# Sums of squares on VectorE, moved transposes, gates and loads, and unread matmuls in two seams of a two-block transformer kernel

## What is computed

```
# block 1
u = rmsnorm(x); p_fox, p_rwkv = u @ w_in
mix = [forgetting_attention(p_fox), rwkv7_time_mix(p_rwkv)] @ w_out
h = x + rmsnorm(mix);  z = rmsnorm(h)
h = h + rmsnorm((silu(z @ w_gate) * (z @ w_up)) @ w_down)
# block 2
h2 = rmsnorm(h); hq, hf, hi, hg, rq, rk, rv, rg, gate_a, gate_b = h2 @ w_in_2
o_hg  = head_rms(hgrn2(hq, hf, hi, lower_bounds)) * w * silu(hg)      # 8 heads of 128
o_ret = head_rms(retention(rotary(rq), rotary(rk), rv)) * silu(rg)    # 4 heads, values of 512
merged = sigmoid(gate_a) * (o_hg @ w_a) + sigmoid(gate_b) * (o_ret @ w_b)
x = h + merged @ w_out_2
x = x + peer_ffn(rmsnorm(x))       # 16384 experts, 8 x 16 chosen per token
return rmsnorm(x)
```

## Time and profile before

| what | us |
|---|---|
| runs | 3435.29, 3425.33, 3425.12 |
| median | 3425.33 |
| the profiled execution, its own time | 3432.69 |
| its span in the trace | 3430.9 |
| PE busy | 3323.2 (97%) |
| DVE busy | 1903.7 (55%) |
| ACT busy | 1251.6 (36%) |
| DMA | 408 MB, mean 119 GB/s |

### The profile page before, as it was taken

How to read it: one execution, slowest core, us unless ns; L and a number is a source line. 1 busy time by engine, 2 the same in 40 slices (tenths; PEclk the granted TensorE clock), 3 DMA queues, 4 the chain that set the end, 5 groups by cost and what they waited for, 6 DMA issues and landing times.

```text
span 3430.9 us, 50060 instructions
## 1 busy us (share of the span) xinstructions
PE 3323.2 (97%) x18511; PEld 2707.1 (79%) x18511; DVE 1903.7 (55%) x3709; ACT 1251.6 (36%) x1622; POOL 131.7 (4%) x54
## 2 busy tenths in 40 slices
PE   8999999999799999989999999999999999999998
PEld 6676877878577788878878888888887788888886
DVE  4466446442565533342344999988884444444443
ACT  3333233322455333342333333444553333333332
POOL 0000000000000000000000445000000000000000
PEclk9999999999899999999999999999999999999999
DMA  3110013323222222213332444555556655555542
GB/s 135 58 44 2 4 49 98 98 92 98 74 67 73 80 74 73 73 62 98 94 100 80 146 144 141 158 179 183 184 183 220 209 192 194 196 196 193 192 146 80
DMA packets 146028, 408.31 MB, mean 119 GB/s; under 512 B 11224, under 2 KB 43992, under 8 KB 143584
## 3 DMA queue, kind: packets, MB, share of 16 engines
q1 hardware_dynamic: 73520, 265.85, 25.5%
q10 hardware_dynamic: 72368, 140.68, 11.3%
HBM read 337.28 MB, written 69.21 MB: 118 GB/s over the span
## 4 chain that ended last, share of the span: by engine, by line
PE 85%; DVE 11%; ACT 2%; issue 1%; ACTq 1%; DMA 1%; DVEq 0%; SPq 0%
PE bank L333 24%; PE bank L335 23%; PE bank L334 23%; PE bank L929 2%; PE bank L429 2%; PE bank L927 2%; PE bank L362 1%; PE bank L863 1%; ACT arena L970 1%; DVE arena L1961 1%; DVE arena L1924 1%; DVE arena L1925 1%; DVE arena L1927 1%; DVE arena L1959 1%; DVE arena L1926 1%
## 5 line engine op out<-in xcount | busy, mean ns | idle before, releaser
L333 PE MATMUL bank<-xs,ring_hi 128*128 128x512 f32 x2488 | 998.1, 401 | 38.3 <-DVE xs L1454 11.8
L335 PE MATMUL bank<-xs,ring_lo 128*128 128x512 f32 x2488 | 974.3, 392 | 0.0
L334 PE MATMUL bank<-xs,ring_hi 128*128 128x512 f32 x2488 | 973.7, 391 | 0.0
L970 ACT ACTIVATE ring_hi<-ring 128x1024 fp32r<-128x1024 f32 x503 | 531.6, 1059 | 660.8 <-DMA ring<-weights 427.0
L970 ACT ACTIVATE arena<-bank 128x512 f32<-128x512 f32 (+4 forms) x584 | 392.0, 705 | 1013.5 <-PE bank L335 727.4
L1488 DVE TENSOR_TENSOR ring_lo<-ring,ring_hi 128x1024 fp32r<-128x1024 f32 x246 | 299.9, 1224 | 566.0 <-ACT ring_hi L970 564.9
L333 PEld LDWEIGHTS bank<-xs,ring_hi 128*128 128x128 f32 x2488 | 470.4, 189 | 149.8 <-issue 27.0
L335 PEld LDWEIGHTS bank<-xs,ring_lo 128*128 128x128 f32 x2488 | 469.8, 189 | 101.6
L334 PEld LDWEIGHTS bank<-xs,ring_hi 128*128 128x128 f32 x2488 | 471.0, 189 | 99.9 <-issue 5.5
L1974 DVE TENSOR_TENSOR ring_lo<-ring,ring_hi 128x1024 fp32r<-128x1024 f32 x206 | 252.3, 1225 | 385.7 <-ACT ring_hi L970 385.7
L333 PE MATMUL bank<-gw,ring_hi 128*128 128x512 f32 x1024 | 398.5, 389 | 0.7 <-ACT arena L970 0.7
(11 more groups left out here) (279 smaller groups left out, 3391.2 us busy)
## 6 DMA issues: line engine op xcount, KB each, us to landing
ring<-weights SPq DMA_DIRECT2D x503, 512.0 KB, 3.6
hidden<-arena ACTq DMA_DIRECT2D x128, 256.0 KB, 4.1
gates<-arena ACTq DMA_DIRECT2D x16, 2048.0 KB, 6.7
arena<-hidden ACTq DMA_DIRECT2D x16, 2048.0 KB, 10.4
arena<-gates ACTq DMA_DIRECT2D x16, 2048.0 KB, 17.2
xres<-x_t ACTq DMA_DIRECT2D x4, 512.0 KB, 6.8
out_t<-arena SPq DMA_DIRECT2D x4, 512.0 KB, 3.0
arena<-ret_decay ACTq DMA_DIRECT2D x1, 1024.0 KB, 5.6
```

The lines of the kernel that those rows point to most:

```text
L333: pe.matmul(out_, wh, x[0], start=start, stop=False, skip_group_check=True)
L334: pe.matmul(out_, wh, x[1], start=False, stop=False, skip_group_check=True)
L335: return pe.matmul(out_, wl, x[0], start=False, stop=stop, skip_group_check=True)
L970: return act.activation(out_, in_, f, **kw)
```

## The change

1. *Sums of squares on DVE.* For norms 0, 1, 3 and 5 (`ACC`) DVE adds the squares (`add_square`) in a third buffer and PE does a single sum (`added_sum`). The same in retention: squares go to `SQ` and, in turn, two buffers at `SQ2`; DVE adds them between its splits of blocks 11 to 13, and one sum stands behind product 11. The values use banks 7 and 5 in turn, values 0 and 1 stand together before product 9, values 2 and 3 before products 10 and 11.
2. *Start.* Products 0 and 1 come before the sum of norm 0; the splits of blocks 2 and 3 stand ahead of the reciprocal.
3. *Fox loop.* The transposes of `TA` and `TB` for pairs 0 to 2 move from the late chain into units 19, 20, 23, 24, 27, 28, with ACT's copies one unit later. Ten tiles stay late; counters that named 36 now name 30.
4. *Seams.* `seam_clock` puts 12 unread matmuls behind the sum of norm 1 and 16 behind that of norm 4.
5. *Lower bounds.* Their softmax stands at the start of the down stage instead of behind it, on DVE and ACT.
6. *Merge.* The sigmoids of the first two gates and the splits of blocks 3 and 4 stand at copies 9 and 14 of the 24.
7. *Loads.* The four transfers stand before blocks 4, 5, 7 and 9 of the rest of U; that loop is unrolled.

The diff, without the renumbered counters:

```diff
+        ACC = {0: 62, 1: 73, 3: 20, 5: 20}
...
+            def seam_clock(n, b, count):
+
+                r = n % RING
+                for _ in range(count):
+                    pe.matmul(bank[b][:, :], ring_hi[:, r, 0:P], ring_hi[:, r, 0:T], start=True, stop=True, skip_group_check=True)
...
+            def added_sum(i):
+
+                pe.wait_ge(sq_used, (KD - 1) * (i + 1))
+                pe.matmul(bank[SUMS[i]][:, :], cc("ones"), tile(ACC[i]), start=True, stop=True,
+                          skip_group_check=True).then_inc(sum_ready, 1)
...
             for n in range(N_FOX):
                 product(n, [(n, KD)], XS, chunk_wait=xs_chunks(0) if n == 0 else None)
-                if n == 0:
+                if n == 1:
                     pe.wait_ge(in_cst, 16)
-                    norm_sums(0, KD)
+                    added_sum(0)
...
+                if u in (19, 20, 23, 24, 27, 28):
+                    i, g0 = (u - 19) % 4, (u - 19) // 4
+                    pe.wait_ge(rw_dve, 2 * g0 + 2)
+                    if 2 * g0 + i:
+                        pe.wait_ge(tok_out, 2 * g0 + i)
+                    for g in range(TT):
+                        tr = pe.transpose(bank[1][:, g * P:(g + 1) * P], tile((TA, TB)[i] + g0)[:, g * P:(g + 1) * P], cc("ident"))
+                    tr.then_inc(tok_ready, 1)
                 if u in (17, 21, 25, 29):
                     pe.wait_ge(rw_dve, 2 * m + 1)
+                    if m:
+                        pe.wait_ge(tok_out, 2 * m)
                     pe.matmul(bank[1][:, :], cc("bones"), tile(RKR), start=True, stop=True).then_inc(rw_pe, 1)
...
-            for i, (src, _) in enumerate(((TA, MA), (TB, MB), (TK, MK), (RV, MV))):
-                for m in range(NPAIR):
-                    j = 4 * i + m
+            pe.wait_ge(tok_out, 2 * (NPAIR - 1))
+            late = [(TA, 3), (TB, 3)] + [(TK, m) for m in range(NPAIR)] + [(RV, m) for m in range(NPAIR)]
+            for j, (src, m) in enumerate(late):
                     if j >= 2:
...
-                for k in {4: (0, 1), 5: (2, 3), 7: (4, 5, 6, 7)}.get(b, ()):
-                    norm_sum(1, k)
+            added_sum(1)
+            ready(B_FFN)
+            seam_clock(B_FFN, 5, 12)
...
-                if k:
-                    norm_sum(3, k - 1)
-            norm_sum(3, KD - 1)
+            added_sum(3)
             norm_sums(4, KD)
+            ready(B_HG)
+            seam_clock(B_HG, 5, 16)
...
+                def values(j):
+
                     if j == 0:
                         pe.wait_ge(rt_dve, h * 12 + 1 + 8)
                         pe.wait_ge(rt_act, h * 9 + 4)
...
+                    if j >= 2:
+                        pe.wait_ge(rt_act, h * 9 + 4 + j - 1)
+                    b = bank[(7, 5)[j % 2]]
...
+
+                product(q + 8, [(B_RET + 8, KD)], XS, h, 12, 12)
+                values(0)
+                for j in range(1, 4):
+                    values(j)
+                    product(q + 8 + j, [(B_RET + 8 + j, KD)], XS, h, 12, 12)
+                pe.wait_ge(rt_sum, h * 4 + 4)
+                pe.matmul(bank[4][:, :], cc("ones"), tile(R_["SQ"]), start=True, stop=True).then_inc(rt_pe, 1)
...
-                if k:
-                    norm_sum(5, k - 1)
...
                 if k == 0:
-                    norm_sum(5, KD - 1)
+                    added_sum(5)
...
+                added = i in ACC
+                if k >= 2 + added:
+                    act.wait_ge(sq_used, (KD - 1) * i + k - 1 - added)
+                elif i and k < 2:
                     act.wait_ge(root_used, i)
-                A(tile(NORM[i][0] + k % 2), src(k), ACT.Square).then_inc(sq_ready, 1)
+                A(tile(ACC[i] if added and k == 0 else NORM[i][0] + k % 2), src(k), ACT.Square).then_inc(sq_ready, 1)
...
+            dense(3)
             norm_root(0)
-            for n in range(3, N_FOX):
+            for n in range(4, N_FOX):
...
+                if u in (20, 21, 24, 25, 28, 29):
+                    i, g0 = (u - 20) % 4, (u - 20) // 4
+                    act.wait_ge(tok_ready, 2 * g0 + i + 1)
+                    A(tile((MA, MB)[i] + g0), bank[1][:, :], ACT.Copy).then_inc(tok_out, 1)
...
             act.wait_ge(ffn_pair, KF + 2)
+            act.wait_ge(lb_ready, 1)
+            A(lbt[:, 1:3, :], lbt[:, 1:3, :], ACT.Exp).then_inc(lb_ready, 1)
...
+                def gate(j):
+
                     act.wait_ge(block_used, h * 12 + B_RET + 8 + j + 1)
                     A(tile(R_["G"] + j), bank[(q + 8 + j) % NBANK][:, :], ACT.Silu).then_inc(evac, 1)
                     dense(B_RET + 8 + j + 3, h, 12)
-                    act.wait_ge(rt_pe, h * 16 + 8 + 2 * j + 1)
-                    st.go(A(arena[:, bass.ds(h * 4 + (ORET + j), 1), :].rearrange("p a t -> p (a t)"), bank[7][:, :], ACT.Copy))
-                    A(tile(R_["SQ"]), bank[7][:, :], ACT.Square).then_inc(rt_act, 1)
...
+                gate(0)
+                for j in range(4):
+                    b = bank[(7, 5)[j % 2]]
+                    act.wait_ge(rt_pe, h * 13 + 8 + j + 1)
+                    st.go(A(arena[:, bass.ds(h * 4 + (ORET + j), 1), :].rearrange("p a t -> p (a t)"), b[:, :], ACT.Copy))
+                    if j >= 2:
+                        act.wait_ge(rt_sum, h * 4 + j)
+                    A(tile(R_["SQ"] if j == 0 else SQ2 + j % 2), b[:, :], ACT.Square).then_inc(rt_act, 1)
+                    if j:
+                        gate(j)
...
+            def merge_gate(j):
+
+                act.wait_ge(block_used, B_MERGE + j + 1)
+                A(tile(MGT + j), bank[(q + j) % NBANK][:, :], ACT.Sigmoid).then_inc(evac, 1)
+                dense(B_MERGE + j + 3)
 
             for k in range(24):
                 if k == 9:
                     act.wait_ge(rt_dve, 12 * RET_H + 1)
+                    merge_gate(0)
+                if k == 14:
+                    merge_gate(1)
                 A(OHL[k][0], tile(OHG + k), ACT.Copy).then_inc(o_hi_ready, 1)
+            q += 2
...
-            def load(g, it=0):
+            def load_part(g, part, it=0):
 
...
-                if g > 1:
-                    act.wait_ge(ex_lo, it * 2 * JG + (g - 1) * JG)
...
+                if part == 0:
...
+            def load(g, it=0):
+
+                act.wait_ge(ex_lo, it * 2 * JG + (g - 1) * JG)
+                load_part(g, 0, it)
+                load_part(g, 1, it)
...
-            load(0)
-            load(1)
-            with act.Fori(1, NU_REST // 4 - 1) as i:
-                for b in range(4):
-                    expert_hi(n + b, i, 4)
-                    gelu(B_U + j0 + b, q + b, j0 + b, i, 4)
+            for b in range(4, NU_REST - 4):
+                if b in (4, 5):
+                    load_part(0, b - 4)
+                if b in (7, 9):
+                    load_part(1, (b - 7) // 2)
+                expert_hi(n + b)
+                gelu(B_U + j0 + b, q + b, j0 + b)
...
+            def add_square(i, k):
+
+                ve.wait_ge(sq_ready, KD * i + k + 1)
+                if k > 1:
+                    ve.wait_ge(sq_used, (KD - 1) * i + k - 1)
+                TTN(tile(ACC[i]), tile(ACC[i]), tile(NORM[i][0] + k % 2), ALU.add).then_inc(sq_used, 1)
...
             dense(1)
+            dense(2)
+            for k in range(1, KD):
+                add_square(0, k)
+            dense(3)
...
+            for n in range(B_WOUT + 4, B_FFN - 1):
                 dense(n)
-            for b in range(3):
-                dense(B_FFN + b)
+            for k in range(1, 4):
+                add_square(1, k)
+            dense(B_FFN - 1)
+            dense(B_FFN)
+            dense(B_FFN + 1)
+            add_square(1, 4)
+            add_square(1, 5)
+            dense(B_FFN + 2)
+            add_square(1, 6)
+            add_square(1, 7)
...
+            for b in range(1, 3 * KD):
+                dense(B_DOWN + b + 3)
+                if b % 3 == 1 and b > 4:
+                    add_square(3, (b - 4) // 3)
...
+            st.sync()
+            add_square(3, KD - 1)
+            norm_add(3, "ffn_post", lambda k: tile(MO[3] + k))
...
+                for j in range(4):
+                    dense(B_RET + 10 + j, h, 12)
+                    ve.wait_ge(rt_act, h * 9 + 5 + j)
+                    if j:
+                        ve.wait_ge(rt_sum, h * 4 + j)
+                        TTN(tile(R_["SQ"]), tile(R_["SQ"]), tile(SQ2 + j % 2), ALU.add).then_inc(rt_sum, 1)
+                    else:
+                        ve.sem_inc(rt_sum, 1)
+                dense(B_RET + 14, h, 12)
...
             for k in range(24):
+                if k in (9, 14):
+                    dense(B_MERGE + (3 if k == 9 else 4))
...
-                for b in range(3, 8):
+                for b in range(3 if k else 5, 8):
...
+                if k > 1:
+                    add_square(5, k - 1)
+            add_square(5, KD - 1)
```

86 lines of the change are left out of this document (35 added, 51 removed).

## The result

The changed kernel took 3393.82 us (median of four runs, 3393.16 to 3395.98), the kernel before 3429.5 in the four runs beside them (3425.12 to 3435.29). The ratio is 0.9892, with a 95% interval of 0.9880 to 0.9905, so about 36 us less. Forecast were 3369.9 us, 55.4 less, and a range from 3353 to 3392. The sign was right; the gain came to two thirds of what I had summed, and the time lies 1.8 us above the range. Part of the gap is the anchor: the three runs that I had had a median of 3425.33, and later sets of seven to nine runs of the same kernel gave 3430.8 to 3432.3.

The account below looks back on a forecast made before the run. It took PE (TensorE), 85% of the chain that ended last, to bound the kernel. Nine terms summed to -55.4 us, taking the median from 3425.33 to 3369.9 us, with a range from 3353 to 3392.

Parts of the forecast that it names:

- the fox loop's: Fox loop: six moved transposes cost 8.8 us in the units, the shorter late chain gives back 4.0, net +4.8.
- B: Fox loop: the moved transposes hide under PE's waits on DVE's maximum, so their 8.8 us vanish; 3361.1 us, chance 0.14.
- C: Loads: they keep PE waiting since the bytes stay, so the 11.0 us gain is lost; 3380.9 us, chance 0.17.
- D: Retention: the new order holds its products, so the 15.4 us gain is lost; 3385.3 us, chance 0.08.
- Start: Kernel start: product 1 follows product 0, one sum replaces eight, product 2 starts at 25.96 instead of 33.90; -7.9 us.
- Down: FFN down stage: six sums between products go, the last sum waits for DVE's last add; -4.5 us.
- Seam before HGRN2: Seam before HGRN2: with the lower-bound softmax taken out, DVE's reciprocal follows norm 4's root sooner; -2.5 us.
- Retention: Retention: one sum instead of four per head, and the last sum's wait for ACT's square hidden; -15.4 us.
- Loads: Four 2 MB loads: spread out, none blocks ACT in its issue and PE's idle time there goes; -11.0 us.
- w_out2: w_out2 stage: six sums leave, 5.16 us, and the last sum ends about with the first query product; -5.0 us.
- Merge: Merge: PE's 9.21 us wait and slow matmuls behind it go, against two new waits; -8.4 us.
- The w_out seam: Seam from w_out to the FFN: root earlier by 3.05 us, unread matmuls keep the clock for 2.5; -5.5 us.

Follow-up runs that it names:

- e7: Changed kernel with the second moved transpose of each group in a free bank behind the RKR matmul, so none waits for ACT's copy of the other: 3368.9 us, ratio 0.9811.
- e4: Changed kernel with 35 unread matmuls ahead of product 2, so all that follows comes about 8 us later: 3400.2 us.
- e5: Kernel before with only the move of six TA and TB transposes into the fox loop: 3451.5 us against 3432.3.
- e1: Changed kernel with the move alone undone, all 16 tiles transposed behind the fox loop: 3374.8 us.
- e11: Changed kernel with the four 2 MB loads in a row again at b = 4: one execution, local shift 11.0 us later behind the loads.
- e16: e1 with three unread matmuls behind each eighth of unit 13's head sums: 3368.6 us.
- e15: Changed kernel with only pair 0's transposes moved, in one bank with the waits, those of pairs 1 and 2 late: 3383.0 us.

## Why the prediction missed

**The step that failed is the fox loop's.** I wrote "That makes 2.5 to 3 us in each of three groups; following PE, ACT and DVE unit by unit with the durations of the trace I get 8.8". The mechanism in it was right: both waits are there, at the places named, and PE's waits at them sum to 6.6 us (e7 removes them). But the durations of the trace were those of the full clock, and the change took that clock away: the term that I had at 8.8, the moved work in the units, measured 25.7 (25.8 in e4, 22.6 in e5). The upper bound that I gave, 8.8, was the forecast itself. Beyond it lay what rows 8 and 3 had already shown for two other places, that matmuls run at half pace behind a wait, and the window of before over 231 to 242 us, low without any wait at all, could have warned me. I charged the low clock at three places where a wait went, and at none where a wait came. Measured, the stretch came out 27.9 longer in the traces, and the move was worth 19 us in the medians (e1, e5): 23 and 14 more than my net 4.8. Of the 23, 16.9 are this term; 6.1 are the longer first low stretch, which begins ahead of the moved work, is there in e7 too, and has no known cause.

**No rival had it.** B bet on less in this loop, C and D on two other places. Both of these were forecast well, and the range, made of their prices, ended 1.8 us under the result. A rival "the new waits bring the lower clock to the rest of the loop" had 38 us to act on, from unit 20's scores at 257.37 to the late transposes at 295.11. If the work in only half of them takes twice its time, that is 19 us and a time of 3389 (an estimate after the fact), and a range with its bound in it ends past the 3393.8.

**The anchor.** The median of three runs, 3425.33, was 4 to 7 us below that of later, larger sets; my own profiled execution, 3432.69, had said so. I carried the difference to the lower number.

**Right, step by step.** Start -7.9 for -7.9. Down -5.5 for -4.5: a sum between products is worth 0.91 rather than 0.86, since the two matmuls behind it also start quicker, and DVE's last add, 0.7, lies behind the border and so in the next term. Seam before HGRN2 -3.0 for -2.5: the reciprocal comes 2.55 nearer to the root, as put; +0.7 is that add, and -1.1 are the eight sums of norm 4, of which fewer lie at the lower clock. Retention -16.4 for -15.4. Loads -11.3 for -11.0, confirmed by e11. (The 0.89 of the window in the working is 6.8 us at the lower level; the 1.8 that I called its length is about what it cost.)

The Trainium skill (DMA: Bandwidth & Descriptors, "Issuing engines are not separate DMA queues") calls the time that it takes to start a DMA usually small beside the transfer. Here it was not: ACT stood 9.72 us in one issue of a transfer that takes 10.4 us from issue to landing in the median, and PE waited for ACT's next copy; spread out, the same bytes made PE wait for nothing, so the gain did not shrink as rival C has it.

**Right in part by luck.** w_out2 -5.3 for -5.0: seven sums left the products, not six, which is -6.4 in the trace, and the last sum cost 1.1 more where I had 0.2; the two errors nearly cancel. Merge -7.6 for -8.4: of the two new waits only the first came (2.15), and a low stretch behind it cost 1.6 in place of the second's 0.8. The w_out seam -8.1 for -5.5: 3.2 of it is a low stretch of the kernel before at 436 to 443 that was absent, which no part of the change aimed at; without it the seam gave 5.0.

## What to carry to other kernels

When work is moved into a loop in which PE is nearly full, a new wait of 1 us is to be priced twice: once as itself, and once as the lower clock over what follows, here 7 to 27 us each time. Look for the bank, buffer or order that makes the wait vanish (here a second PSUM bank, worth 25 us between the medians, where the move itself could gain 4.0) before counting the gain of the move. And where every duration of a working comes from rows at the full clock, its result is the lower end, not both ends, of the range. To see which part of a stretch went wrong, compare the starts of instructions that both kernels have: the medians of e1 and e5 said 19 us, and only the traces split off the 6.1 that the move had not caused.

## What the runs showed of the hardware

- The same kernel differs from run to run by up to 23 us (e1: 3366.4 to 3389.4), and the mean granted clock goes with it: 0.992 at the lower end and 0.984 at the upper. A difference of under 0.5% between two such kernels needs many runs, or the local comparison of two traces.
- Waits are not all alike. In e16, PE is busy 20.77 of the 24 us from 264 to 288 with the clock at 1.00 throughout; in e15, a wait of 1.30 us (to 249.54) is followed by 27 us at the lower level from 252.3. None of e16's waits in its loop is longer than 0.75 us, but one of 1.48 us among the RWKV chunks (to 299.71) is not followed by a fall either. So neither the length of a wait nor the sum of the waits decides alone, and no run explains what does.
- The clock can stay low while PE's row has no gap at all: 24.00 of 24.00 us busy at 0.51 in the changed kernel from 222 to 246 us, 48 us on end in e1. PE's work there is the loop's mixture of scores (64 rows), masks (8 rows), 128x128 transposes and values, and one unread 128x512 in most units; whether that is the reason was not settled.
- A blocked issue: the third 2 MB transfer in a row holds ACT for 9.72 us (before) and 9.18 (e11), while with 5 to 11 us between the issues it takes 0.40 (2627.15 in the changed kernel).
